# Opening of a hybrid decode layer: x on one DMA queue, the index projection's first tile divided by tokens at 256

## What is computed

```python
h = einsum('btd,dc->btc', x, w_in)          # 7248 columns
q, k, v, ga, qi, ki, wi, u, gb = split(h)   # ki: 64 columns, wi: 16 columns
qi, ki = rope(qi), rope(ki)
s = einsum('bthd,bsd->bths', qi, ki)        # 16 index heads of width 64
I = einsum('bths,bth->bts', relu(s), wi) * scale
idx = top_k(causal(I), 128 or 256)          # the keys that each query attends to
a = attend(q, k[idx], v[idx])
p = pool_mix(u)
y = LayerNorm(alpha * x + W_out [silu(ga) * a ; silu(gb) * p])
```

## Time and profile before

| | |
|---|---|
| Median of 3 runs | 1159.78 us (1159.22 to 1161.22) |
| Profiled execution, first to last instruction | 1156.5 us |
| PE busy in it | 1125.3 us, 97% |
| DVE, POOL, ACT busy | 56%, 32%, 28% |
| Granted TensorE clock, mean | 0.988 |
| Chain that ended last: PE / DVE / DMA | 91% / 5% / 1% |

### The profile page before, as it was taken

One profiled execution on the slowest core, in us unless ns is written; L12 is line 12 of the kernel. 1 busy time (PEld: TensorE's weight loads), 2 busy tenths in 40 slices (PEclk: granted clock), 3 DMA queues, 4 the chain that ended last, 5 costly groups with the idle time before them and its releaser, 6 DMA issues.

```text
span 1156.5 us, 29684 instructions
## 1 busy us (share of the span) xinstructions
PE 1125.3 (97%) x11836; PEld 1048.8 (91%) x11836; DVE 642.4 (56%) x1184; ACT 327.0 (28%) x605; POOL 372.6 (32%) x158
## 2 busy tenths in 40 slices
PE   6999999999999999999999899999999999999995
PEld 5988889999999999999998898988988899999993
DVE  3566666897547556754266574555546443232455
ACT  5233234323332322233232221221212332122330
POOL 2322332233234333433441313221322233343660
PEclk8999999999999999999999999999999999999997
DMA  8543232333233323335423888887978684233333
GB/s 261 136 107 87 61 100 70 84 94 91 74 93 96 82 83 91 84 83 166 124 57 110 270 314 287 312 285 258 350 243 286 219 287 132 74 89 91 111 97 149
DMA packets 208039, 175.86 MB, mean 152 GB/s; under 512 B 20114, under 2 KB 188874, under 8 KB 206706
## 3 DMA queue, kind: packets, MB, share of 16 engines
q1 hardware_dynamic: 194554, 165.72, 46.3%
q10 hardware_dynamic: 13376, 8.53, 2.4%
HBM read 164.29 MB, written 10.03 MB: 151 GB/s over the span
## 4 chain that ended last, share of the span: by engine, by line
PE 91%; DVE 5%; issue 2%; DMA 1%; ACT 0%; DVEq 0%; SPq 0%; ACTq 0%
PE acc L1166 68%; PE acc L1148 4%; PE acc L1530 3%; PE bank L1467 3%; PE bank L1224 2%; PE bank L1360 2%; PE bank L1341 2%; PE acc L1583 2%; DVE scoreP L1830 1%; DVE top L1826 1%; PE acc L1494 1%; DMA xnat<-in_x_prompt 1%; PE bank L1276 1%; PE bank L1350 1%; DVE y L2262 1%
## 5 line engine op out<-in xcount | busy, mean ns | idle before, releaser
L661 POOL TENSOR_TENSOR wL<-rawW,wH 128x1024 fp32r<-128x1024 f32 (+1 forms) x154 | 372.4, 2420 | 749.7 <-ACT wH L683 749.7
L1166 PE MATMUL acc<-actH,wH 128*128 128x272 f32 (+1 forms) x2176 | 466.6, 296 | 1.0 <-DVE actL L1744 1.0
L1166 PE MATMUL acc<-actH,wL 128*128 128x272 f32 (+1 forms) x2176 | 451.2, 289 | 0.0
L1166 PE MATMUL acc<-actL,wH 128*128 128x272 f32 (+1 forms) x2176 | 450.2, 288 | 0.0
L1166 PEld LDWEIGHTS acc<-actH,wH 128*128 128x128 f32 (+1 forms) x2176 | 341.2, 188 | 31.1 <-issue 29.6
L1166 PEld LDWEIGHTS acc<-actL,wH 128*128 128x128 f32 (+1 forms) x2176 | 342.5, 189 | 0.0
L1166 PEld LDWEIGHTS acc<-actH,wL 128*128 128x128 f32 (+1 forms) x2176 | 340.4, 189 | 0.0
L683 ACT ACTIVATE wH<-rawW 128x1024 fp32r<-128x1024 f32 (+1 forms) x154 | 161.6, 1053 | 260.6 <-PE acc L1166 232.2
L1782 DVE SCALAR_TENSOR_TENSOR scoreP<-relu,wiN,scoreP 128x256 f32<-128x256 f32 (+2 forms) x54 | 45.3, 879 | 33.4 <-ACT relu L740 33.4
L1935 DVE STREAM_TRANSPOSE kPage<-kPage 128x1024 f32<-128x1024 f32 x30 | 37.1, 1237 | 40.3 <-DMA kPage<-in_cache_k 39.4
L2178 DVE SCALAR_TENSOR_TENSOR y<-y,bank 128x512 f32 x12 | 8.3, 688 | 89.8 <-PE bank L1647 86.6
(11 more groups left out here) (226 smaller groups left out, 1072.1 us busy)
## 6 DMA issues: line engine op xcount, KB each, us to landing
rawW<-in_w_in SPq DMA_DIRECT2D x112, 512.0 KB, 3.8
vPage<-in_cache_v SPq DMA_DIRECT2D x64, 512.0 KB, 6.8
kPage<-in_cache_k SPq DMA_DIRECT2D x60, 512.0 KB, 5.3
rawW<-in_w_out SPq DMA_DIRECT2D x40, 512.0 KB, 4.0
y<-in_x_prompt SPq DMA_DIRECT2D x4, 1024.0 KB, 8.0
out_y_prompt<-y SPq DMA_DIRECT2D x8, 512.0 KB, 2.7
xnat<-in_x_prompt SPq DMA_DIRECT2D x2, 1024.0 KB, 7.9
xnat<-in_x_prompt ACTq DMA_DIRECT2D x2, 1024.0 KB, 11.6
```

The source lines that it names most:

```text
L661: pool.tensor_tensor(wL[:, slot, :, 0:width], rawW[:, slot, :, 0:width], wH[:, slot, :, 0:width].bitcast(F32), ALU.subtract).then_inc(stag ...
L1166: last = pe.matmul(acc[t.slot][0:width, e, 0:HT], w[:, u.slot, k, 0:width], a[:, kk, e * HT:(e + 1) * HT], start=(half == 0 and k == 0 and ...
```

## The change

Five edits, all in the opening:

1. SP issues x0, x1, x2, then the index tile's two units, then xnatS, then x3. ACT issues only `sq` and the two small tables.
2. The index tile's units are loaded 128 columns wide, so in pieces of 512 bytes. ACT and POOL still split 80 columns.
3. The blocks are turned in the order x0, x1, x2, xnatS, x3 (`TURNED`) by PE, ACT and DVE alike. ACT makes the index weights' high parts one before xnatS and one before x3.
4. The index tile is computed in two parts by tokens: 0 to 255 (part 0) and 256 to 543 (part 1), in four pieces of 24 matmuls. The first half of part 0 stands ahead of the turning of x3, everything else behind it. The wL products of each piece come after its 16 wH products.
5. The two parts lie side by side in PSUM (`kiwi`, a row of 544), and ACT copies them out in one piece.

```diff
@@ -81,6 +81,8 @@
 TWICE = 4
 WHOLE = KC - TWICE
 EARLY_T = 2 * P
+TURNED = (0, 1, 2, 4, 3)
+FIRST_T = 2 * P
 RT = 4 * 12
 RS = RT + 6
 WT = 20
@@ -373,7 +375,8 @@
 
 
         banks = Banks((*four, OUT, SIDE))
-        xb = banks.stage([f"x{t}{q}" for t in range(TT + 1) for q in range(4)], four)
+        xb = banks.stage([f"x{t}{q}" for t in TURNED for q in range(4)], four)
+        kiwi = acc[0][:].rearrange("p e t -> p (e t)")[:, 512 - FIRST_T:512 - FIRST_T + T]
         ab = banks.stage(["wi"], four)
 
         def rt(place):
@@ -454,10 +457,12 @@
                 for half in range(2):
                     load_unit(view, half if tile < TILE_D else 1 - half, col, turn(2 * tile + half, 4, i, 2 * per))
 
-            for t in range(2):
+            for t in range(3):
                 sp.dma_start(xnat[:, t, :], x_prompt[0, t * P:(t + 1) * P, :]).then_inc(x_in[t], 16)
             for half in range(2):
-                load_unit(w_view, half, KI0, turn(half, 4), KW)
+                load_unit(w_view, half, KI0, turn(half, 4))
+            sp.dma_start(xnatS[:], x_sample.rearrange("b t d -> (b t) d")).then_inc(xs_in, 16)
+            sp.dma_start(xnat[:, 3, :], x_prompt[0, 3 * P:4 * P, :]).then_inc(x_in[3], 16)
             sp.dma_start(pageT[:], page_table.rearrange("(a b) c -> a (b c)", a=1)).then_inc(pages_in, 16)
             sp.dma_start(s_pool[0, :, 0:HIST - NT, :], state_pool[0, :, NT:HIST, :]).then_inc(spool_sent, 16)
             sp.wait_ge(pages_in, 16)
@@ -481,7 +486,7 @@
                     load_tile(w_view, QI0 + (2 * i + j) * P, TILE_A + j, i, 2)
 
                     for q in range(4):
-                        b = xb(f"x{TT}{q}")
+                        b = xb(f"x{TURNED[-1]}{q}")
                         sp.wait_ge(bank_free[b.slot], b.read)
                     for p in range(BESIDE):
                         index_page(2 * BESIDE * i + (BESIDE * j + p))
@@ -697,17 +702,13 @@
                 act.activation(dst, src, ACT.Copy).then_inc(bank_free[b.slot], 1)
 
             act.dma_start(sq[:], square).then_inc(square_in, 16)
-            for t in range(2, TT):
-                act.dma_start(xnat[:, t, :], x_prompt[0, t * P:(t + 1) * P, :]).then_inc(x_in[t], 16)
-            act.dma_start(xnatS[:], x_sample.rearrange("b t d -> (b t) d")).then_inc(xs_in, 16)
             act.dma_start(headrot[:], head_rot).then_inc(consts_in, 16)
             act.dma_start(halfscale[:], pool_scale[0].rearrange("(j p) -> p j", p=P), allow_slow_non_contiguous=True).then_inc(consts_in, 16)
 
 
-            for t in range(TT + 1):
-                if t == TT:
-                    for half in range(2):
-                        high(0, half, width=KW)
+            for t in TURNED:
+                if t in TURNED[3:]:
+                    high(0, TURNED.index(t) - 3, width=KW)
                 n = P if t < TT else NS
                 for q in range(4):
                     b = xb(f"x{t}{q}")
@@ -716,16 +717,16 @@
                                    src.rearrange("p (k t) -> p k t", k=4), ACT.Copy).then_inc(x_high, 1)
 
             for q in range(4):
-                b = xb(f"x{TT}{q}")
+                b = xb(f"x{TURNED[-1]}{q}")
                 act.wait_ge(bank_free[b.slot], b.read)
             act.dma_start(irot[:], idx_rot).then_inc(irot_in, 16)
 
 
             high(1, 0)
             high(1, 1)
-            src, copied = projected(0)
-            act.activation(halves(wiT[ID:KW, :]), src[ID:KW], ACT.Copy, scale=ISCALE)
-            act.activation(halves(kiT[0:ID, :]), src[0:ID], ACT.Copy).then_inc(copied, 1)
+            copied = projected(0)[1]
+            act.activation(wiT[ID:KW, :], kiwi[ID:KW], ACT.Copy, scale=ISCALE)
+            act.activation(kiT[0:ID, :], kiwi[0:ID], ACT.Copy).then_inc(copied, 1)
             high(2, 0)
             act.wait_ge(ki_ready, 1)
             act.dma_start(kiT[ID:P, :], kiT[0:ID, :]).then_inc(ki_twice, 16)
@@ -1184,7 +1185,8 @@
 
 
             pe.wait_ge(square_in, 16)
-            for t in range(TT + 1):
+            def x_turned(t):
+
                 n = P if t < TT else NS
                 if t < TT:
                     pe.wait_ge(x_in[t], 16)
@@ -1198,13 +1200,37 @@
                         last = pe.transpose(dst[:, j * n:(j + 1) * n], src[:, (4 * q + j) * P:(4 * q + j + 1) * P],
                                             ident[0:n, 0:n])
                     full(b, last)
-            for q in range(4):
-                b = xb(f"x{TT}{q}")
+
+            def x_split(t, q):
+                b = xb(f"x{t}{q}")
                 pe.wait_ge(bank_free[b.slot], b.read)
 
-
-            for half in range(2):
-                unit(0, half, width=KW)
+            def index_part(e, half):
+
+                cols = slice(0, FIRST_T) if e == 0 else slice(FIRST_T, T)
+                dst = kiwi[0:KW, cols]
+                slot, read = half, turn(half, 4).read
+                pe.wait_ge(high_ready[slot], 1)
+                for w, parts in ((wH, (actH, actL)), (wL, (actH,))):
+                    if w is wL:
+                        pe.wait_ge(stage_ready[slot], read)
+                    for k in range(HU):
+                        if k % 4 == 0 and w is wH:
+                            x_split(1 if e == 0 else 3, 2 * half + k // 4)
+                        for a in parts:
+                            last = pe.matmul(dst, w[:, slot, k, 0:KW], a[:, half * HU + k, cols],
+                                             start=(half == 0 and k == 0 and w is wH and a is actH),
+                                             stop=(half == 1 and k == HU - 1 and w is wL))
+                if e == 1:
+                    last.then_inc(stage_free[0] if half == 0 else tile_ready[0], 1)
+
+            for t in TURNED[:4]:
+                x_turned(t)
+            index_part(0, 0)
+            x_turned(TURNED[4])
+            index_part(0, 1)
+            index_part(1, 0)
+            index_part(1, 1)
 
             def index_weights_turned():
                 b = ab("wi")
```

## The result

The changed kernel is slower: 1167.05 us (1162.86 to 1168.08, 6 runs) against 1159.5 us for the kernel before (1157.81 to 1162.56, 6 runs). The ratio is 1.0057, 95% interval 1.0043 to 1.0071, so 5.0 to 8.2 us. The forecast was 1161.3, with a range up to 1164.6. The forecast was thus 1.5 us above the kernel before; by the ratio 6.6 came. The mechanism that it names is there, link by link, and the loss is four to five times as large.

A forecast was written before the change was run, and what follows sets the result against it. The prediction took PE, busy 97% of the span, as the bound. Dense work moved by +0.5 us and +1.0 of clock made a span of 1158.0; 3.3 to the median gave 1161.3 us, range 1157.6 to 1164.6.

The forecast's parts named there:

- What is late next: SP's pages behind x's last split delay tile 3's unit, so tile 1's first rectification is 3.0 to 3.1 us late.
- S: Time in the opening when the first 24 index matmuls end and x3's turning starts on PE; forecast 22.4 us.
- S + 27.6: Forecast time at which ACT can start tile 1's first rectification, which is wanted at S + 24.5.
- The last split at S + 3.9: DVE's last split of x3 comes 3.9 us after S; 72 index matmuls hide it, ending the tile at S + 11.1.
- The sum: Net change of the span: +0.5 us in PE's dense work and +1.0 of clock, +1.5 in all, 1158.0 against 1156.5.
- S - 21.9: Shift of PE's dense work from tile 1's fifth product on; +0.5 us with S = 22.4.
- the same count and shapes: The forecast's reason for letting DVE's work cost nothing more after the change; no size was added.
- The second drop of the clock: Half clock on PE behind the 3.5 us wait in tile 1's products; between 0 and 2.7 us, taken as +1.0.
- Line rate from 512 bytes up: Skill's rule for the wide index units' transfer: 0.8 us sooner and total 0.8 less; the forecast stayed with 316 GB/s.
- (a): Rival: pages and tile 3's unit aren't late, PE's gain of 2.5 to 4.4 us stays, 1155.4 to 1157.3; chance 0.12.
- (b): Rival: half clock from the wait ahead of xnatS, S 25.5 or more, +5.0 with second drop, 1164.8; 0.14 with another rival.
- the forecast's own case: Stall in tile 1's products and partial loss of clock; 1158.0 to 1164.0 with S from 20.1 to 23.5; chance 0.74.

The follow-up runs named there:

- the fastest version: Kernel with pages released by x2's split, x3 before the sampled tokens, 80-column units, both high parts behind x2, page table on ACT; 1156.06 us, 0.9969 to the kernel before.

## Why the prediction was right and wrong

- **What is late next: right.** The first page went 1.3 us after x3's last split (28.7 to 30.05), tile 3's units 19.1 after it (18.7 were forecast), and the first rectification at 52.72, where S + 27.6 gives 52.4. Releasing the pages earlier, or holding them in the old kernel, makes the loss go and come.
- **The last split at S + 3.9, and the index matmuls behind it: right.** It was 28.72 with S = 24.77. The index tile at full clock behind x3 was as long as worked out.
- **The sum.** The span was forecast 1.5 us longer and is 9.1 longer. Of the 7.6 us between, 2.4 are in S, 0.3 in the queue, 1.7 in DVE's adds beside POOL, 2.0 in the clock behind the stall and 1.2 later on, where the clock dips more.
- **S itself: the first term that was mis-sized.** 22.4 was forecast, 24.77 came, so S - 21.9 was 2.9 us instead of 0.5. Of the 2.4, 1.7 is the clock: I took a third of the way between full and half, 3.5 us for the 24 matmuls, and they ran at half and took 5.2 (19.57 to 24.77). The prediction had PE's wait of 2 us ahead of them in hand, and it was 2.95. 1.0 is the sampled tokens, at 17.96 and not 17.0, and their turning gave 0.3 back. In that landing time the 0.6 us from the last byte to PE is a term that no run shows by itself; what the runs show is that the wide units put 1.25 us on it.
- **A cost that wasn't in the sum: POOL.** I let tile 3's unit be late for ACT and went straight on to the rectification, and dismissed DVE with "the same count and shapes". But with the high part made just ahead of it, POOL's low part lies beside DVE's first adds, 1.7 us on the path. At this place the trace of before had nothing of it, since tile 3's low part was over. But it had it one tile later: two adds of the same shape took 2.87 us beside a low part at 60.14, so this step of the chain, the one that was left out, could have been read from it.
- **The second drop of the clock: mis-sized.** 1.0 us was taken between 0 and 2.7, and 3.0 came. The wait before it was 5.6 us and not 3.5, and the granted clock is 0.50 in the rows from 54 to 62. The rule of the Trainium skill on waits between bursts (TensorE: Matmul & The Clock Gate, HAM oscillation), by which the drop was certain, was right here: both long waits of this trace were followed by half clock, and with the gap filled the index matmuls ran at full. But the rows don't give a length of wait that decides it. At the fifth product waits of 0.47 and 1.19 us were followed by the full clock and those of 1.62, 1.63 and more by a lower one, while in the opening of the kernel before the granted clock is 1.00 from 19.5 to 20.0 and 0.50 from 20.25 on, ahead of the 1.00 us wait there and behind waits of no more than 0.2 us in PE's transposes.
- **Line rate from 512 bytes up** (the Trainium skill, DMA: Bandwidth & Descriptors, Specifications) changed nothing for the better here: 2048 pieces of 320 bytes (0.66 MB) were through earlier than 2048 of 512 (1.05 MB).
- **The rivals.** (a), that the queue isn't in the way, fell. (b), slower by the clock, is what happened on top of the forecast's own case: the prediction priced the stall, the drop in the opening and the second drop each alone, and gave their sum 0.14. They hang together. A late S makes the stall not longer but later, the stall makes the drop sure, and POOL lengthens it. The price of (b), 1164.8, already lay above the range, which was too narrow for all three together. The upper end of the forecast's own case is a slip too: S = 23.5 and a drop of 2.4 give 1163.8, not 1164.0.

## To carry to other kernels

When a step is moved later, look for every engine that waits for its *end*, not only for the one whose work is to gain; here a wait for "x is all split" guarded memory that most of the pages behind it didn't even use. Count how many issues stand between that wait and the next thing that the busy engine needs, since a queue of at least 1.3 us a page, as here, is a clock of its own. And when two engines' delays meet, add their interference and the lower clock behind the gap to the same case, not as separate chances.

## What the runs showed of the hardware

- DVE's multiply-add with two inputs in SBUF: 1.01 us for two alone, 2.68 beside one POOL subtraction of 2.34 us that also reads SBUF.
- PE at half clock through 24 index matmuls behind a wait of 2.95 us, and at full clock through the same matmuls when 24 extra transposes filled it. The 5.56 us wait at 55.57 has a granted clock of 0.50 in the rows of 54 to 62 around and behind it, and 0.91 in 62 to 66. At the same product a wait of 1.62 us (the pages released by x2, with the fill) was followed by 0.57 from 50 to 54, one of 1.19 (x3 ahead of the sampled tokens) or 0.47 by 1.00. In the opening of the kernel before, the clock fell from 1.00 to 0.50 between 20.0 and 20.25 with no wait over 0.2 us since 11.4.
- The index units' 2048 pieces took longer at 512 bytes (1.05 MB) than at 320 (0.66 MB): 1.25 us on the next transfer.
- SP's issues: 1.3 us for each page that is addressed from the page table, in most groups of every trace (six in 6.8 us), and more where an issue is held up: the first six took 9.23 us in the fastest version, one of them 2.73 by itself.
